# Attention on one core: rotary partners 64 rows apart, v twice side by side, and another order of the steps ahead of the scores

## The reference

```python
qkv = h @ w_qkv + b_qkv          # 32 query heads, 4 key heads, 4 value heads, 64 wide
q, k = rope(q, pos), rope(k, pos)
# rope, per head: x1, x2 = the two halves of 32 columns
#   out = concat([x1 * cos - x2 * sin, x2 * cos + x1 * sin])
# each chunk of 64 tokens sees its own chunk and the one before
scores = einsum('bcqkgd,bcskd->bckgqs', q, k_band) * 64 ** -0.5   # invalid: -1e30
probs = softmax(concat([scores, sink]))[..., :-1]
out = einsum('bckgqs,bcskd->bcqkgd', probs, v_band)
return out @ w_o + b_o
```

## Time and profile before

| | us |
|---|---|
| median of 3 runs | 2025.28 |
| lowest, highest | 2025.14, 2028.07 |
| the profiled execution's own time | 2027.66 |
| its span, first to last instruction | 2025.7 |
| TensorE busy in the span | 1999.9 |
| VectorE busy | 1358.7 |
| ScalarE busy | 1057.6 |

### The profile page before, as it was taken

The page is one execution under the profiler, slowest core; times in us unless marked ns, Lnnn a source line. Parts: engine busy times, 40 slices in busy tenths (PEclk is TensorE's granted clock), DMA queues, the critical chain, the costliest instruction groups (busy, mean ns, idle before and its releaser), DMA issues.

```text
span 2025.7 us, 34215 instructions
## 1 busy us (share of the span) xinstructions
PE 1999.9 (99%) x11604; PEld 1747.6 (86%) x11604; DVE 1358.7 (67%) x1560; ACT 1057.6 (52%) x1438; POOL 8.7 (0%) x12
## 2 busy tenths in 40 slices
PE   9999999999999999999999999999999999999997
PEld 8888888888888888888888888888888888888886
DVE  7777676656655665667688887666566556656665
ACT  7555454444444444445588885544444444444453
POOL 1000000000000000000000000000000000000000
PEclk9999999999999999999999999999999999999998
DMA  8433556556565655565655555565566556555652
GB/s 276 141 104 115 195 169 207 190 184 193 180 197 177 199 190 188 180 195 175 209 178 185 180 166 183 176 207 187 186 186 187 195 178 197 187 188 178 202 171 90
DMA packets 365879, 368.12 MB, mean 182 GB/s; under 512 B 11536, under 2 KB 363920, under 8 KB 365712
## 3 DMA queue, kind: packets, MB, share of 16 engines
q1 hardware_dynamic: 365552, 365.53, 57.0%
q0 software_dynamic: 288, 2.10, 0.3%
HBM read 365.48 MB, written 2.10 MB: 181 GB/s over the span
## 4 chain that ended last, share of the span: by engine, by line
PE 90%; DVE 5%; ACT 2%; issue 2%; DMA 0%; DVEq 0%; ACTq 0%; SPq 0%
PE ps L1256 58%; PE ps L1259 29%; DVE w_lo L766 2%; PE aux L1276 1%; PE aux L1277 1%; PE aux L1278 1%; DVE xc L1145 0%; ACT L616 0%; DVE u L780 0%; PE aux L1292 0%; DVE v L1102 0%; PE aux L1329 0%; DMA h<-x_l_dram 0%; DVE h L1241 0%; ACT w_hi L343 0%
## 5 line engine op out<-in xcount | busy, mean ns | idle before, releaser
L766 DVE TENSOR_TENSOR w_lo<-w_raw,w_hi 128x1024 fp32r<-128x1024 f32 x678 | 816.7, 1223 | 336.3 <-ACT w_hi L343 335.2
L343 ACT ACTIVATE w_hi<-w_raw 128x1024 fp32r<-128x1024 f32 x678 | 701.7, 1054 | 434.7 <-PE ps L1259 432.1
L1256 PE MATMUL ps<-xn,w_hi 128*128 128x512 f32 x2880 | 908.4, 397 | 3.7 <-DVE xn L834 2.3
L1256 PE MATMUL ps<-mid,w_hi 128*128 128x512 f32 x2544 | 800.8, 396 | 1.9 <-DVE mid L903 1.5
L1259 PEld LDWEIGHTS ps<-xn,w_lo 128*128 128x128 f32 x2880 | 541.8, 188 | 128.3
L1259 PEld LDWEIGHTS ps<-mid,w_lo 128*128 128x128 f32 x2544 | 478.7, 188 | 113.2
L1259 PE MATMUL ps<-xn,w_lo 128*128 128x256 f32 x2880 | 566.7, 278 | 0.0
L1259 PE MATMUL ps<-mid,w_lo 128*128 128x256 f32 x2544 | 500.5, 278 | 0.0
L1256 PEld LDWEIGHTS ps<-xn,w_hi 128*128 128x128 f32 x2880 | 439.4, 189 | 5.8 <-issue 5.1
L1256 PEld LDWEIGHTS ps<-mid,w_hi 128*128 128x128 f32 x2544 | 388.0, 189 | 2.6 <-issue 2.6
L780 DVE TENSOR_TENSOR u<-ps,half 128x512 f32<-128x512 f32 x170 | 117.4, 691 | 182.9 <-ACT half L356 160.9
(11 more groups left out here) (154 smaller groups left out, 808.2 us busy)
## 6 DMA issues: line engine op xcount, KB each, us to landing
w_raw<-mlp_w_up_dram SPq DMA_DIRECT2D x256, 512.0 KB, 3.8
w_raw<-mlp_w_down_dram SPq DMA_DIRECT2D x256, 512.0 KB, 3.4
w_raw<-b_w_in_dram SPq DMA_DIRECT2D x64, 512.0 KB, 4.9
w_raw<-a_w_qkv_dram SPq DMA_DIRECT2D x40, 512.0 KB, 5.2
w_raw<-a_w_o_dram SPq DMA_DIRECT2D x32, 512.0 KB, 3.7
w_raw<-b_w_out_dram SPq DMA_DIRECT2D x32, 512.0 KB, 4.4
h<-x_l_dram SPq DMA_DIRECT2D x4, 512.0 KB, 8.5
gate_raw<-b_gate_a_w_dram SPq DMA_DIRECT2D x8, 256.0 KB, 2.8
```

Source lines behind the costliest of these rows:

```text
L343: nc.scalar.activation(w_hi[:, s, :, :], w_raw[:, slot, :, :], ACT.Copy).then_inc(hi_ready, 1)
L766: nc.vector.tensor_tensor(w_lo[:, s, :, :], w_raw[:, slot, :, :], w_hi[:, s, :, :].bitcast(F32), ALU.subtract).then_inc(lo_ready, 1)
L1256: nc.tensor.matmul(ps[:, 2 * half_i + b, :], hi[:, k, b * PART:(b + 1) * PART], operand[:, :, kt, :], start=kt == 0, stop=False)
```

## The change

Five things change.

1. The columns of q and k are permuted outside the kernel (`_halves_apart`), so that the first halves of two heads lie on rows 0 to 63 and the second halves on rows 64 to 127. A row's rotary partner is then 64 rows away. `rope` on VectorE reads the partner's rows directly: one instruction of 128 rows for cos, two of 64 rows for sin, which read rows 64 to 127 and write rows 0 to 63 and the other way round, and the addition. `rotate` on TensorE is gone for all nine calls; one matmul of the same form, `swap_keys`, stays for the keys.
2. The padded keys are written by four instructions of 128 rows with a 0/1 factor per row, where there were two copies and four instructions of 64 rows.
3. `vcur` holds v twice side by side (128 columns), so `attend` needs 12 matmuls of 256 columns where there were 24 of 128. Its result takes two PSUM banks, and comes out with the two heads' rows apart, so `att_hi` and `att_lo` are two instructions of 64 rows and 512 elements each.
4. `xs` moves to PSUM banks 0 and 1 of `aux`, and the output of `attend` to banks 2 and 3.
5. The order: `rope` of a pair is done a step earlier, behind `softmax_scale` of the pair two before it; `q_split_lo` comes ahead of `pt_split_lo`, `roped_hi` ahead of `pt_split_hi`, and `att_lo` moves from its place ahead of `softmax_scale` to the end of the step.

On VectorE, the back part of the second step of the loop and the front of the next one, before: `h<-h 128x1024` is the scaling of the probabilities, `w_lo` the split of a weight chunk, the three with `h` and `const` or 512 the rope, `pt` and `qz` the two splits.

The diff, cut to what is spoken of:

```diff
-        x0, xs, x3 = aux[:, 0, :], aux[:, 1:3, :], aux[:, 3, :]
+        x0, xs, x3 = aux[:, 0, :], aux[:, 0:2, :], aux[:, 3, :]
+        att_out = aux[:, 2:4, :].rearrange("p x (c b a t) -> p (x c) b a t", c=2, b=2, a=2)
...
             def att_hi(j):
                 act.wait_ge(att_done, j + 1)
-                nc.scalar.activation(mid[:, 0, bass.ds(j * 2, 2), :], x0.rearrange("p (b t) -> p b t", b=2),
-                                     ACT.Copy).then_inc(att_out_hi, 1)
+                for a in range(2):
+                    r = slice(HD * a, HD * a + HD)
+                    last = nc.scalar.activation(att_place(0, j)[r], att_out[r, :, :, a, :], ACT.Copy)
+                last.then_inc(att_out_hi, 1)
...
                 next_hi(q, half_i, 0)
+                roped_hi(j)
                 pt_split_hi(j - 1)
-                roped_hi(j)
...
                 copy_half(q, half_i)
+                q_bias(j + 1)
                 att_hi(j - 1)
-                q_bias(j + 1)
                 next_hi(q, half_i, 3)
...
-            def rope_cos(n):
+            def rope(n):
                 dve.wait_ge(rope_in, n + 1)
-                nc.vector.tensor_tensor(qa, u[:, :, :], bc2(cos), ALU.mult).then_inc(cos_done, 1)
-            def rope(n):
-                dve.wait_ge(rotated, n + 1)
-                nc.vector.tensor_tensor(qb, x3.rearrange("p (b t) -> p b t", b=2), bc2(sin), ALU.mult
-                                        ).then_inc(rot_read, 1)
-                dve.wait_ge(cos_done, n + 1)
-                dve.wait_ge(rot_read, n + 1)
+                nc.vector.tensor_tensor(qa, u[:, :, :], bc2(cos), ALU.mult).then_inc(rope_terms, 1)
+                for src, dst in ((slice(HD, PART), slice(0, HD)), (slice(0, HD), slice(HD, PART))):
+                    nc.vector.tensor_tensor(qb[dst], u[src, :, :], bc2(sin[src], HD), ALU.mult).then_inc(rope_terms, 1)
+                dve.wait_ge(rope_terms, n * 3 + 3)
                 nc.vector.tensor_tensor(qa, qa, qb, ALU.add).then_inc(roped, 1)
...
             def attention_step(q, half_i, j):
-                rope_cos(j + 1)
-                rope(j + 1)
+                q_split_lo(j)
                 pt_split_lo(j - 1)
-                q_split_lo(j)
                 if half_i == 0:
                     vcur_split_lo(q - 2)
                 next_lo(q, half_i, 0)
...
                 next_lo(q, half_i, 2)
                 qkv_scale(q, half_i)
+                softmax_scale(j)
+                rope(j + 2)
+                next_lo(q, half_i, 3)
                 att_lo(j - 1)
-                softmax_scale(j)
-                next_lo(q, half_i, 3)
...
+                p_hi, p_lo = (pt[:, part, :, :].rearrange("p b (a c t) -> p c b a t", a=2, c=4) for part in range(2))
                 for c in range(4):
-                    out = x0.rearrange("p (b t) -> p b t", b=2)[:, :, c * HD:(c + 1) * HD]
-                    for a in range(2):
-                        v_cols = slice(HD, 3 * HD) if a == 0 else slice(0, 2 * HD)
-                        p_cols = slice(a * TOK + c * HD, a * TOK + (c + 1) * HD)
-                        last = three(out, vcur[:, 0, c, v_cols], vcur[:, 1, c, v_cols],
-                                     pt[:, 0, :, p_cols], pt[:, 1, :, p_cols], a == 0, a == 1)
+                    last = three(att_out[:, c], vcur[:, 0, c, :], vcur[:, 1, c, :], p_hi[:, c], p_lo[:, c], True, True)
...
-            pair(1, 0, *qkv, {0: lambda: rotate(0), 2: transpose_v})
+            pair(1, 0, *qkv, {1: swap_keys, 2: transpose_v})
```

More of the change, by code:

```diff
@@ L477, in _ @@
             next_hi(1, 0, 0)
+            qkv_bias(1, 18, vt[:, 0, HD:HD + TOK], vt[:, 1, HD:HD + TOK], vt_ready)
+            next_hi(1, 0, 1)
+            act.wait_ge(zeros_set, 3)
             act.wait_ge(roped, 1)
[L479 to L482, removed]
             act.wait_ge(kswapped, 1)
[L484 to L487, removed]
+            for head, side, src in key_places:
+                last = nc.scalar.activation(key_out(0, head, side), src, ACT.Copy, scale=head_rows[:, side:side + 1])
             last.then_inc(k_hi, 1)
-            for s in range(1, 3):
-                next_hi(1, 0, s)
+            next_hi(1, 0, 2)
             copy_half(1, 0)
+            q_bias(0)
             next_hi(1, 0, 3)
-            q_bias(0)
             next_hi(1, 1, 0)
@@ L927, in _ @@
             dve.wait_ge(const_loaded, 16)
-            rope_cos(0)
             rope(0)
@@ L985, in _ @@
             last = PAIRS - 1
-            rope_cos(last + 1)
-            rope(last + 1)
             next_lo(QB_WO, 0, 0)
@@ L1285, in stats, with swap_keys @@
                                  ).then_inc(stats_done, 1)
-            def rotate(n):
-                pe.wait_ge(rope_in, n + 1)
-                nc.tensor.matmul(x3, swap, u[:, :, :], start=True, stop=True).then_inc(rotated, 1)
+            def swap_keys():
+                pe.wait_ge(roped, 1)
+                nc.tensor.matmul(x3, swap, qa, start=True, stop=True).then_inc(kswapped, 1)
             def transpose_v():
@@ L1366, in attention_pair @@
             def attention_pair(q, half_i, j, g, g_before):
[L1368 to L1369 removed]
+                between = {2: lambda: scores_and_output(j, g, g_before)}
+                if g_before is not None:
+                    between[1] = lambda: transpose_probs(j - 1)
+                pair(q, half_i, *qkv, between)
             attention_pair(1, 1, 0, 0, None)
@@ L1450, in _rope_tables, with _halves_apart @@
     cos = np.cos(ang).astype(np.float32).T[p % half]
-    sin = np.sin(ang).astype(np.float32).T[p % half] * np.where(p % HD < half, -1.0, 1.0)[:, None]
+    sin = np.sin(ang).astype(np.float32).T[p % half] * np.where(p < HD, 1.0, -1.0)[:, None]
     swap = np.zeros((PART, PART), np.float32)
     swap[p, p ^ half] = 1.0
-    return np.concatenate([cos, sin, swap, np.eye(PART)], axis=1).astype(np.float32)
+    head = (p // half) % 2
+    rows = np.stack([head == 0, head == 1], axis=1)
+    return np.concatenate([cos, sin, swap, np.eye(PART), rows], axis=1).astype(np.float32)
+def _halves_apart(a):
+    heads = a[..., :(HEADS + KV_HEADS) * HD]
+    pairs = heads.reshape(*heads.shape[:-1], -1, 2, 2, HD // 2).swapaxes(-3, -2)
+    return np.concatenate([pairs.reshape(heads.shape), a[..., heads.shape[-1]:]], axis=-1)
 def _columns(a):
```

68 lines of the change are left out of this document (35 added, 33 removed).

## The result

The changed kernel took 2042.39 us (median of four runs, 2040.54 to 2043.22), the kernel before 2026.67 beside it. The ratio is 1.0078, with a 95% interval of 1.0062 to 1.0094: slower by 0.8%, some 15.7 us. The forecast was slower, at 2033.5 with a range of 2024.5 to 2039. The direction came out, and half of the size; the time lies 3.4 us above the range. The profiled execution took 2041.72 us with a span of 2039.9, against 2027.66 and 2025.7 before.

What follows compares the result with a forecast made beforehand. A ring of work through VectorE, ScalarE and VectorE was taken to bound each step. Stage terms of -0.5 us, +7.3 for clock falls ahead of scores and +1.4 at the output projection gave 2033.5 us, range 2024.5 to 2039.

Steps and rivals of the forecast that it cites:

- The ring: Attention loop: work through VectorE, ScalarE and VectorE from one pair's scores to the next, below which no step can go.
- 0.60 is the distance between 512-wide instructions: VectorE's part of the ring: the price taken for each added 512-wide instruction, 0.60 us.
- 18.78 us: Attention loop: the ring's length after the change, 0.20 us less than the step of 18.98 before.
- seven falls and 0.3 us more: Top of the range: 7 drops of TensorE's clock and 0.3 us more in each step, given as 2039.
- The idle time and the clock: TensorE ahead of scores: gaps of 2.1 us (pair 1: 1.7) lower the clock, 1.33 us more per step, 7.3 in all.
- The ends: Attention stage outside the five steps: +0.18 us at pair 1's scores, +0.66 at pair 7, -0.35 after the last scores.
- The last stretch: After the last scores: attend of pair 7 earlier and shorter, att_hi and att_lo longer, -0.35 us.
- The clock stays up: Rival, TensorE: no clock fall behind gaps of 2 us, only behind the 3.3 us one; +0.9 us, 2026.2; chance 0.2.
- Half rows cost half: Rival, VectorE: the two sin and two att_lo take 0.30 us each, ring 17.58, some 2016.5 us; chance 0.08.
- Crossing rows costs a second pass: Rival, VectorE's sin instructions: +1.2 us per step on top of the forecast, six times, 2041 us; chance 0.05.
- `attend` isn't shorter: Rival, TensorE: 256-column matmuls might cost 0.22 us each, list 17.7, gap 0.9, no clock fall, 2026 us; chance 0.05.

Runs made afterwards that it cites:

- e1_filler: The changed kernel with ten small useless float32 matmuls on TensorE ahead of the scores of pairs 1 to 6; 2033.36 us, ratio 1.0026.
- e2: The changed kernel with att_lo moved from its step's end to behind the next step's pt_split_lo, except pair 5's; 2028.54 us, ratio 1.0009.
- e3: e2 with w_lo of chunk 3 behind the next step's pt_split_lo and w_lo of chunks 0 and 1 behind softmax_max; 2023.01 us, ratio 0.998.
- e7: e3 with pt_split_hi ahead of roped_hi on ScalarE and pt_split_lo ahead of q_split_lo on VectorE; 2020.45 us, ratio 0.9966.
- e10: e7 with ScalarE's w_hi of chunk 0 moved behind pt_split_hi and roped_hi; 2017.94 us, ratio 0.9955.
- e6_old_order: The changed kernel with the old order of the steps on ScalarE and VectorE; 2039.07 us, ratio 1.0061.
- e9_one_sin: e1_filler with six small matmuls in place of ten and the two sin instructions merged to one of 128 rows, rotation wrong; 2024.93 us, ratio 0.9988.
- e5_rope_old_order: The rope and keys part of the change alone, with v as in the kernel before and the old order of steps; 2027.68 us, ratio 1.0003.
- e11_v_only: The kernel before with the v part of the change alone, rotate kept but behind the transposes; 2028.45 us, ratio 1.0008.
- e8: e7 with pair 5's att_lo moved ahead of the rope in the last step; 2021.71 us, ratio 0.9965.

## Why the prediction was half right

**The ring sets the step: right, and shown.** e1_filler holds TensorE's clock and gives steps of 19.42 us with TensorE's list at 18.8; e2, e3, e7 and e10 take out what stands in the ring and the step follows. While VectorE doesn't wait from the addition of q to `pt`, the order of its instructions is of no weight (e6_old_order: 0.1 us). Where VectorE waits there for ScalarE, the order counts: e7 and e10 gained by it.

**The ring's length, the step that failed: "0.60 is the distance between 512-wide instructions", and with it "18.78 us".** The ring measured 19.42 where the clock stayed up, 0.64 more. The distance of the earlier trace rows is that of instructions that overlap by 0.08, and most of those added don't. By item, forecast and measured after: rope 2.60 and 2.76 (129.82 to 132.58); the two `att_lo` 1.20 and 1.41 (133.72 to 135.13); `q_split_lo` 0.60 and 0.73 (to 135.86); `pt` to the scores 1.38 and 1.50. These are 0.62 of the 0.64. From cos to sin, from sin to the addition, from `mid` to `q_split_lo` and from there to `pt` the next one starts 0.02 to 0.04 us behind the end of the one before. For the addition this has nothing to do with the halves: it waits for its own terms, and in e9_one_sin, with a whole sin, it starts 0.04 behind it as well (142.89, 142.93); the forecast had that wait. For the first sin half e9 shows the cause. For the splits, VectorE's timelines of three kernels in which `pt_split_lo` stands behind the addition and ahead of `q_split_lo`: e6_old_order (`att_lo` in halves), e5_rope_old_order (whole) and e11_v_only (in halves, but the sin at L872 reads all rows of `aux` behind them):

```profile
133.28 0.69 DVE L873 TENSOR_TENSOR h<-h 128x512 f32<-128x512 f32 x1
134.01 1.23 DVE L904 TENSOR_TENSOR pt<-aux,pt 128x1024 fp32r<-128x1024 f32 x1
135.15 0.68 DVE L878 TENSOR_TENSOR qz<-h,qz 128x512 fp32r<-128x512 f32 x1
```

```profile
130.31 0.69 DVE L870 TENSOR_TENSOR h<-h 128x512 f32<-128x512 f32 x1
130.92 1.22 DVE L901 TENSOR_TENSOR pt<-aux,pt 128x1024 fp32r<-128x1024 f32 x1
```

```profile
129.32 0.69 DVE L876 TENSOR_TENSOR h<-h 128x512 f32<-128x512 f32 x1
129.93 1.22 DVE L907 TENSOR_TENSOR pt<-aux,pt 128x1024 fp32r<-128x1024 f32 x1
```

In e6 `pt` starts 0.04 behind the addition's end (133.97), in e5 and e11 0.08 ahead of it (131.00 and 130.01). And in e6 `qz`, which is held in the changed kernel, starts 0.09 ahead of `pt`'s end (135.24). So `pt` has no overlap where the last instruction that read PSUM took rows 64 to 127, even with SBUF instructions in between, and has it where all rows were read last.

The Trainium skill has a rule for this ("VectorE: DVE Perf Modes", section "Two Vector instructions with no wait between them"), which I hadn't used: an instruction is held until all earlier ones have finished if one of its inputs starts at another quarter of the rows than the first input of the last instruction that read the same memory, or if its output starts at another quarter than the last output into its memory. The traces agree: by it the `att_lo` of rows 64 to 127 holds `qz` by its SBUF operands and `pt` by PSUM, the sin of e11 lifts the latter, and each of the starts measured here is as it says.

Over the five steps the 0.64 make 3.2 us, the largest part of the miss in the spans. It turned a ring of 0.2 less than before into one of 0.44 more. The whole miss on the medians is 8.9 us: 6.0 in the profiled spans (14.2 against 8.2), 1.4 because the median of the kernel before rose from 2025.28 to 2026.67 with its fourth run, and 1.5 between the medians and the profiled executions. The top of the range was also added up loosely: seven falls and 0.3 us more in each of seven steps come to 2037.6 by the prediction's own terms, not 2039.

**The idle time and the clock: right in kind and in sum, not one by one.** Gaps of 2.1 were forecast (1.7 at pair 1), and 2.5 to 2.8 measured (2.12). The forecast had a fall behind nearly each. The first had none, the other five did, and in one of them the lower clock lasted twice as long (the step of 21.78). That these two offset each other is luck. Together they cost 8.4 - 5 x 0.44 = 6.2 us in the five steps, against 6.0. The chunk behind the 3.49 us gap took 4.16 us (198.63 to 202.79) and not 2.80: 1.4, as forecast.

**The ends.** Pair 1's scores came 0.9 later than forecast. 0.44 was there at the scores of pair 0 already (57.92 against 57.48), which I took as 0 within 0.3; with profiles that have them anywhere from 56.4 to 59.4, this can't be put down to the change. The way from pair 0 to pair 1 took 0.4 more than forecast (18.59 us against 18.00 before), which is the ring's items again. The last stretch missed by 0.6.

**The rest of the span**, 0.9 us, lies outside the change. In the recurrent stage the lower clock lasted twice as long as in the profile of before. It did so in the profiles of e1, e2, e5, e6, e8, e9 and e10 as well, but not in those of e3 and e7, which hold the change too, nor in that of e11. What decides it isn't shown.

**The rivals.** *The clock stays up*: false, by the windows at 0.50, and e1_filler prices it; the page's rule of the Trainium skill on idle gaps ("TensorE: Matmul & The Clock Gate", section "Why this matters for your kernels") would have the clock stay up at these gaps, and the trace disagrees at 2.5 to 2.8 us, where it fell behind all five, and at the other end too, with no fall behind 3.52 us in e1_filler. *Half rows cost half*: false, 686 ns. *Crossing rows costs a second pass*: false, the sin halves cross and take the same 686 ns. *`attend` isn't shorter*: false; its 12 matmuls take 0.36 us for three (205.67 to 206.03 in the tail), 1.44 in all.

## What to carry to other kernels

Where the busiest engine waits a little each round, add up the ring from one of its waits to the next, over all engines, before taking work off it. What is saved there comes back as idle time until something leaves the ring. Reordering one engine's instructions inside the ring gives nothing while it never waits there; moving what nobody waits for to where the ring is on another engine does, and so does an order in which two engines' parts of the ring run beside each other. A saving can go below zero: idle time on TensorE may cost its clock, and the work right behind the gap, which stands in the ring, pays.

Price an instruction that is put between others by its full duration, and check separately that it overlaps; 64 rows cost as much as 128.

## What the runs showed of the hardware

- On VectorE, instructions of 128 rows that follow each other without a wait overlap by 0.08 us. Where the first works on rows 64 to 127, or the next one starts there, there is no overlap but 0.01 to 0.04 us between them (L869 to L871, L911 to L878). A read of rows 64 to 127 of PSUM still held `pt`, the next to read PSUM, eight SBUF instructions later (e6_old_order), and a whole read of PSUM in between freed it (e11_v_only). An instruction that waits for the result of the one ahead of it starts 0.03 to 0.04 us behind it (L871 to L873, and L870 to L872 in e9_one_sin).
- The clock's fall isn't set by a gap's length alone. Behind 2.12 us at 76.52 there was none, nor behind 2.82 in e8_tail_too, 3.51 in e2_att_off or 3.52 in e1_filler (ahead of the output projection's third chunk). In e6_old_order gaps of 2.28, 1.94 and 1.94 us (76.52, 95.83, 177.57) had none, and gaps of 1.96, 1.94 and 1.96 between the last two had one each. Before the change 1.50 was enough.
- Matmuls of no use kept the clock: float32 ones by ones, 128 columns, 0.24 us each, ten of them in each gap of e1_filler and six in those of e9_one_sin, which left 0.6 us idle.
